# Two small TensorE steps moved one weight slab later each, and one weight split moved ahead of a pair of squares, in a two-layer hybrid block

## The reference

```python
for l in range(DEPTH):                                   # DEPTH = 2
    h = rms_norm(x, norm_mix_g[l])
    pa, pb, pc, pg = jnp.split(h @ w_in[l], GROUP_POINTS, axis=-1)
    oa = rwkv7_time_mix(pa, ...)                         # branch A: a gated delta rule over time, 8 heads of 64
    ob = stick_breaking_attention(pb)                    # branch B: 8 heads of 64
    oc = differential_attention(pc, ...)                 # branch C: 4 heads
    ga, gb, gc = jnp.split(jax.nn.sigmoid(pg), 3, axis=-1)
    merged = ga * (oa @ w_branch_a[l]) + gb * (ob @ w_branch_b[l]) + gc * (oc @ w_branch_c[l])
    x = x + merged @ w_out[l]
    x = x + conv_ffn(rms_norm(x, norm_ffn_g[l]), ...)
return rms_norm(x, norm_final_g)

def stick_breaking_attention(pb):                        # the part called "bz" below
    z = einsum('bhqd,bhkd->bhqk', qb, kb) * scale
    log_skip = where(mask, log_sigmoid(-z), 0)
    later = cumsum(log_skip, axis=3, reverse=True) - log_skip
    A = where(mask, exp(log_sigmoid(z) + later), 0)
    o = einsum('bhqk,bhkd->bhqd', A, vb)
```

## Time and profile before

| | before |
|---|---|
| median of 3 runs | 1031.81 us |
| lowest, highest | 1031.12, 1033.04 us |
| the profiled execution, its own time | 1032.37 us |
| its span | 1030.5 us |
| TensorE (PE) matmul busy | 1012.3 us, 98% of the span |
| VectorE (DVE) busy | 819.7 us, 80% |
| ScalarE (ACT) busy | 618.6 us, 60% |
| DMA, mean over the span | 159 GB/s |
| granted TensorE clock, mean | 0.997 of full |

### The profile page before, as it was taken

The page is one execution under the profiler, slowest core; times in us unless marked ns, Lnnn a source line. Parts: engine busy times, 40 slices in busy tenths (PEclk is TensorE's granted clock), DMA queues, the critical chain, the costliest instruction groups (busy, mean ns, idle before and its releaser), DMA issues.

```text
span 1030.5 us, 22708 instructions
## 1 busy us (share of the span) xinstructions
PE 1012.3 (98%) x8522; PEld 945.8 (92%) x8522; DVE 819.7 (80%) x1371; ACT 618.6 (60%) x967; POOL 11.9 (1%) x30
## 2 busy tenths in 40 slices
PE   8999999999999999999999999999999999999997
PEld 7998988899999999999999989789999999999996
DVE  6799763797797898878778996649968789887876
ACT  7964332656556665766689533246656666666765
POOL 0000000100000000000000000010000000000000
PEclk9999999999999999999999999999999999999999
DMA  8452342335445565555534533233435445555553
GB/s 300 156 173 103 116 150 64 114 111 177 156 157 182 181 206 184 185 190 180 197 131 155 175 111 135 83 90 126 148 141 184 165 164 204 193 192 190 184 185 126
DMA packets 46282, 163.93 MB, mean 159 GB/s; under 512 B 5904, under 2 KB 6080, under 8 KB 46192
## 3 DMA queue, kind: packets, MB, share of 16 engines
q1 hardware_dynamic: 44640, 160.19, 45.0%
q10 hardware_dynamic: 864, 1.63, 0.6%
q0 software_dynamic: 688, 0.81, 0.4%
HBM read 161.04 MB, written 1.05 MB: 157 GB/s over the span
## 4 chain that ended last, share of the span: by engine, by line
PE 85%; DVE 9%; ACT 3%; issue 2%; DMA 1%; SPq 0%; DVEq 0%; ACTq 0%
PE psum L468 84%; DVE sb_lo L1306 2%; ACT sb_rw L916 1%; DMA sb_raw<-w_stream 1%; DVE sb_inv L1555 1%; DVE sb_inv L1514 1%; DVE sb_inv L1517 1%; PE psum L786 1%; ACT sb_hh L916 1%; ACT sb_hi L916 0%; DVE sb_rw L1598 0%; DVE sb_yf L1579 0%; DVE sb_qb L1364 0%; DVE sb_rw L1485 0%; DVE sb_inv L1491 0%
## 5 line engine op out<-in xcount | busy, mean ns | idle before, releaser
L916 ACT ACTIVATE sb_hi<-sb_raw 128x1024 fp32r<-128x1024 f32 (+1 forms) x298 | 310.2, 1052 | 168.6 <-PE psum L468 158.6
L1306 DVE TENSOR_TENSOR sb_lo<-sb_raw,sb_hi 128x1024 fp32r<-128x1024 f32 x296 | 357.9, 1218 | 53.3 <-ACT sb_hi L916 52.9
L468 PE MATMUL psum<-sb_hh,sb_hi 128*128 128x256 f32 x1184 | 344.3, 291 | 2.6 <-DVE sb_lo L1306 1.3
L468 PE MATMUL psum<-sb_o,sb_hi 128*128 128x256 f32 (+1 forms) x1728 | 339.6, 308 | 1.3 <-DVE sb_o L1327 1.3
L468 PE MATMUL psum<-sb_hl,sb_hi 128*128 128x256 f32 x1184 | 335.5, 283 | 0.0
L468 PE MATMUL psum<-sb_hh,sb_lo 128*128 128x256 f32 x1184 | 335.2, 283 | 0.0
L468 PEld LDWEIGHTS psum<-sb_o,sb_hi 128*128 128x128 f32 x1728 | 278.6, 191 | 14.2 <-DVE sb_o L1327 1.7
L468 PE MATMUL psum<-sb_o,sb_lo 128*128 128x256 f32 x1056 | 243.8, 283 | 0.0
L468 PEld LDWEIGHTS psum<-sb_hh,sb_hi 128*128 128x128 f32 x1184 | 227.2, 192 | 17.2 <-issue 10.2
L468 PEld LDWEIGHTS psum<-sb_hl,sb_hi 128*128 128x128 f32 x1184 | 227.4, 192 | 0.7 <-issue 0.5
L468 PEld LDWEIGHTS psum<-sb_hh,sb_lo 128*128 128x128 f32 x1184 | 227.3, 192 | 0.0
(11 more groups left out here) (181 smaller groups left out, 938.0 us busy)
## 6 DMA issues: line engine op xcount, KB each, us to landing
sb_raw<-w_stream SPq DMA_DIRECT2D x299, 512.0 KB, 3.3
sb_pm<-mix_par ACTq DMA_DIRECT2D x2, 512.5 KB, 3.7
y_t<-sb_rw SPq DMA_DIRECT2D x4, 256.0 KB, 2.5
sb_cf<-const_f SPq DMA_DIRECT2D x1, 550.0 KB, 8.6
sb_pm<-mix_par SPq DMA_DIRECT2D x1, 512.5 KB, 9.8
sb_raw<-w_stream SPq DMA_DIRECT2D x2, 256.0 KB, 4.6
sb_x<-x_t ACTq DMA_DIRECT2D x2, 256.0 KB, 4.6
sb_x<-x_t SPq DMA_DIRECT2D x1, 512.0 KB, 6.1
```

What stands on the lines that cost most here:

```text
L468: return pe.matmul(out, lhsT, rhs, start=start, stop=stop, skip_group_check=True)
L916: return act.activation(out, in_, func, scale=scale, bias=bias, **kw)
L1306: tt(lo[:, s, :], raw[:, s, :], hi[:, s, :].bitcast(F32), ALU.subtract).then_inc(lo_done, 1)
```

## The change

On TensorE `natv` moves behind slab 20, so that it stands directly ahead of `natk`, and `bz 0` moves behind slab 43, directly ahead of `bz 1`. ACT's and DVE's lists stay as they are. On ACT, at the beginning of the second layer (the first has no slab split there), the high part of the third slab moves ahead of the last pair of squares, `square(3)`.

```diff
 STEPS = placed(
-    "... D15-18 + D19 +3 D20 +2 D21 +5 D22-23 ..."
-    "... D40 + D41 + D42 + D43 "
-    "+2 D44-45 +2 D46 ..."
+    "... D15-18 + D19 +2 D20 +3 D21 +5 D22-23 ..."
+    "... D40 + D41 + D42-43 + "
+    "+2 D44-45 +2 D46 ..."
@@ ACT, step xs 0
                             for b in range(3):
                                 square(b)
-                        square(3)
                         if l:
                             ahead(l - 1, SLABS - 1)
+                        square(3)
```

## The result

The changed kernel takes 1039.6 us (median of 8 runs, 1036.63 to 1040.88) beside 1032.1 us of the kernel before in runs on the same chip: slower by the factor 1.0068, with a 95% interval of 1.0051 to 1.0085 (written as [1.0051, 1.0085] below; the two medians alone give 1.0073). That is 0.8 us above the top of the range. Its profiled execution took 1038.83 us, with a span of 1037.0 us, 6.5 us more than before.

The account below looks back on a forecast made before the run. TensorE, its matmuls covering 98% of the span, was taken as the bound. natv +0.5 and bz +2.2 us per layer, twice, less 0.52 for the squares, gave +4.9: 1036.7 us against 1031.81, range 1034.4 to 1038.8 us.

Parts of the forecast that it names:

- 2.27 us on L1371: Ahead of slab 46, TensorE would wait some 2.2 us for DVE's copy out of slab 43.
- 1.33 on L652: Ahead of natk, TensorE would idle some 1.4 us for ACT's copies of natv, which free bank 3.
- DVE idle for 2.39 us: Ahead of its scans of the first bz 0, DVE would idle some 2.4 us, where it had nearly none.
- the `bz` part: bz 0 behind slab 43: scores 2.26 us later delay DVE's queue, so TensorE loses 2.2 us per layer at bav 0.
- `bav 0` had 0.44 us of wait: Ahead of bav 0, TensorE would wait 0.6 us for DVE's mask btri 0 (L1623).
- the working's 0.60 us: After both bz steps, slab 44 on TensorE would start 0.60 us earlier, at 194.85 instead of 195.45.
- The third slab lost its wait of 0.56 us: Start of the second layer: high part one square earlier, so the third slab starts 0.52 us earlier, once.
- the sum: Whole kernel: +2.7 us per layer, +5.4 in two, less 0.52 for the squares: +4.9 us.
- The term `natv`: natv behind slab 20: natk 0.94 us late, idle time ahead of dxy takes back 0.46; +0.5 us per layer.
- The sum has no such term: TensorE's clock behind the new 2.2 us stalls: claimed to add nothing, slow clock left to a rival.
- that rival: Slow clock behind the new stalls: half speed in both layers, 1.95 us each, +3.9 on top, 1040.6 us; chance 5%.
- 1 us of scatter: Measured time of the whole kernel: run scatter of 1 us was allowed on top of the forecast's bounds.

Follow-up runs that it names:

- the filled kernels: The changed kernel with two or three matmuls on constants added on TensorE in the gap ahead of slab 46: 1038.99 us with two, 1038.47 us with three.
- nat_bank4: Kernel before with only natv moved behind slab 20 and natk's second half in bank 4 instead of bank 3: 1031.6 us, ratio 0.9999.
- after_again: The changed kernel run once more without edits, against the kernel before: 1038.94 us, ratio 1.0058.
- after_filled2: The changed kernel with three matmuls on constants on TensorE ahead of slab 46, against the kernel before: 1038.47 us, ratio 1.0053.

## Why the prediction was wrong, and where it was right

**Right: what waits, where, and by how much.** The waits are those named, 2.27 us on L1371 (2.2 forecast), 1.33 on L652 (1.4), DVE idle for 2.39 us (2.4) ahead of its scans. In undisturbed layers the `bz` part cost +2.22 us (2.2 forecast), and `bav 0` had 0.44 us of wait (0.6). The gain was larger than the working's 0.60 us: slab 44 starts 0.83 us earlier (195.45 - 194.62), since two `bz` in a row took 1.51 us and not twice 0.86. It changes nothing, as the wait for DVE takes it all. The third slab lost its wait of 0.56 us. The list of waits alone shows 0.54 and 0.35 us to gain; the gain lay on TensorE and the price on DVE's queue, as the working has it. The runs with the highest clock agree: 1036.70 us, the mean of the changed kernel's two, less 1031.85, the mean of before's 45, is 4.85 us; the sum said 4.9. That rests on two runs, and the five runs of the filled kernels at 0.998 have a mean of 1036.97, so the agreement to 0.05 us is luck.

**The term `natv` was a little small.** The step was that the solve's idle time takes back 0.46 of 0.94 us. It vanished, but DVE's masking of `m1` moved behind TensorE and took part of it again: 0.64 and 0.63 us a layer instead of 0.5, and +0.27 in all.

**Wrong: "The sum has no such term".** This is the step that failed: TensorE's clock was put at nothing. The working saw that a half clock behind each new stall couldn't be excluded, and gave it 5% and no place in the range. In the profiled execution it came in both layers and cost 0.96 us each. The size in that rival, 1.95 us each, was too large on three counts. The stretch is 3.4 us, not 3.9; in it matmuls start 0.21 us apart instead of 0.12, so it costs 3.4 x (1 - 0.12/0.21), some 1.4 us, and not half its length; and `bav 0`'s wait for DVE absorbs 0.44 us of it.

The evidence for leaving it out was misread as well. The working says that matmuls started 0.12 us apart once the slow start was over, and that waits up to 0.56 us changed nothing. But the trace of before has a stretch of half clock of its own in the first layer's solve, where the mean granted clock (PEclk) is 0.72:

```profile
156.00:162.00 6.00, 6.00 (x35) 5.21 (x35) 1.57 (x5) 0.00 (x0) 0.00 (x0) 0.72 0.01 3
```

So the clock could fall without a long stall, and the execution that the forecast was built on already held 1.6 us of it. The Trainium skill (TensorE: Matmul & The Clock Gate, HAM oscillation) led the working to leave the term out, since it asks for longer gaps than this; the measurement decides against that reading, with half clock behind 4 of 8 such waits. The same page of the Trainium skill (A second HAM failure mode: psum-queue depth-cycling) also tells of a kernel whose clock swung from frequent short idle times between groups of matmuls alone. The stretches in the solve, where the longest wait of before is 0.7 us, are compatible with that; no run here tests it.

**Wrong: 1 us of scatter.** The three runs shown spanned 2 us; the 70 runs span 1030.67 to 1038.48. Between before's runs at 0.999 and those at 0.994 lie 2.33 us, more than the range's upper arm of 2.1 us. For the changed kernel 2.55 us lie between the mean of its two runs at 0.998 and 1039.25, the median of its 13. That is what the sum lacks, and it could only be read after the runs. (The bounds of the working add up to 1038.6, not to the 1038.8 of the range; the result is above both.)

**What stays open.** That the half clock in slab 46 needs the unfilled gap rests on 4 of 8 layers against 0 of 4, which chance could give. Filling the gap made the timed runs hardly faster: the median of the 16 filled ones is 1038.49 us, 0.8 under that of the changed kernel's 13. So of the 2.55 us that the sum lacks, the half clock in slab 46 is shown to be a part in the profiles, and how large a part it is in the timed runs is open. They record only the clock's mean, not the places.

## What to carry to other kernels

A step's place on one engine is also its place in the queues of all engines that read its result. Before a step is moved later, look for idle time behind its consumer, not ahead of the step: here 0.35 us of gap on TensorE was bought with 2.2 us of a DVE that has no idle time for 11 us from its scans on. Where the bound engine's clock can fall, a forecast should carry the clock as a term of its own, and a spread taken from many runs. Look first for such stretches in the profile that the forecast starts from.

## What the runs showed of the hardware

- TensorE's clock falls to half for 3.4 us at a time in the middle of a kernel whose TensorE is busy for 98% of the span, and not in the same places from one execution to the next. In before's solve such a stretch cost 1.6 us (mean clock 0.72 over 156 to 162 us), behind the wait it cost 0.96. Here is nat_bank4's, where the longest idle time just ahead is 0.41 us:

```profile
155.99 1.14 PE L468 MATMUL psum<-sb_yf,sb_inv 64*64 64x64 f32 x16 [0.41 <-DVE sb_inv L1568]
157.06 1.85 PE L468 MATMUL psum<-sb_rw,sb_inv 128*128 128x64 f32 x8
...
159.67 0.63 PE L468 MATMUL psum<-sb_hi,sb_hl 128*128 128x512 f32 x1
...
161.04 0.39 PE L468 MATMUL psum<-sb_hi,sb_hh 128*128 128x512 f32 x1
```

- The slow start varies too. Before, the half clock ended at 10.57 us; in the changed kernel's profile the matmuls were 0.21 us apart until 13.37, and 0.12 from 13.73 on, which made all that followed 0.97 us late. after_again and after_filled2 had the long start as well. That is 3 of the 4 profiles of the whole change and none of the other 8. The change moves no step before 76 us, so nothing in the order explains it. Whether it is chance stays open: dealt at random over the 12 profiles, three long starts fall on these four in 2% of cases. If it is not chance, up to 1 us of the timed loss lies there.
- A half clock is partly hidden where the next step waits for another engine anyway: the 1.4 us that it added in slab 46 cost 0.96, and the 0.44 us wait on L1623 was gone.
